# Attention output of a hybrid conv/attention block: the halves of V added on VectorE before the transpose, two heads to a transpose

## The reference

```python
xn = rms_norm(x, norm_mix_g[l])
z = jnp.einsum("bsd,dc->bsc", xn, w_in[l])        # B | C | h | q | k | v
...
scores = jnp.einsum("bnqhd,bnkhd->bnhqk", q, k_band) * (HEAD_DIM ** -0.5) + bias
p = jax.nn.softmax(scores, axis=-1).astype(v.dtype)
o = jnp.einsum("bnhqk,bnkhd->bnqhd", p, v_band)
...
y_mix = concat([group_rms_norm(y_conv, conv_out_g[l], 64), group_rms_norm(y_attn, attn_out_g[l], 64)])
x = x + jnp.einsum("bsc,cd->bsd", y_mix, w_out[l])
xn = rms_norm(x, norm_mlp_g[l])
x = x + relu(xn @ w_mlp_in[l]) ** 2 @ w_mlp_out[l]
```

## Time and profile before

| | |
|---|---|
| median of 3 runs | 1128.45 us (1126.46 to 1129.71) |
| the profiled execution | 1128.77 us, of which its span is 1127.0 us |
| granted PE clock | 0.998 of full speed |
| PE busy | 1101.8 us (98%) |
| PEld busy | 918.2 us (81%) |
| DVE busy | 711.4 us (63%) |
| ACT busy | 538.7 us (48%) |
| POOL busy | 628.5 us (56%) |
| share of PE in the chain that ended last | 91% |

### The profile page before, as it was taken

How to read it: one execution, slowest core, us unless ns; L and a number is a source line. 1 busy time by engine, 2 the same in 40 slices (tenths; PEclk the granted TensorE clock), 3 DMA queues, 4 the chain that set the end, 5 groups by cost and what they waited for, 6 DMA issues and landing times.

```text
span 1127.0 us, 14684 instructions
## 1 busy us (share of the span) xinstructions
PE 1101.8 (98%) x5272; PEld 918.2 (81%) x5272; DVE 711.4 (63%) x899; ACT 538.7 (48%) x885; POOL 628.5 (56%) x368
## 2 busy tenths in 40 slices
PE   5999999999999999999999999999999999999998
PEld 5888888888888877887888888888878888888887
DVE  6677757767766785336425353534467767776798
ACT  6664665565466563225454545445453343333330
POOL 4322141230412130167778888787789697796992
PEclk9999999999999999999999999999999999999999
DMA  8311110120110514121454444444676435345324
GB/s 260 99 38 38 40 56 18 37 58 19 56 38 3 187 71 154 54 78 50 166 195 151 149 150 149 151 148 160 241 281 236 149 121 192 134 132 204 112 75 167
DMA packets 98511, 135.79 MB, mean 120 GB/s; under 512 B 8072, under 2 KB 52112, under 8 KB 98456
## 3 DMA queue, kind: packets, MB, share of 16 engines
q1 hardware_dynamic: 95104, 131.13, 34.7%
q10 hardware_dynamic: 3352, 3.94, 1.2%
HBM read 97.27 MB, written 39.34 MB: 121 GB/s over the span
## 4 chain that ended last, share of the span: by engine, by line
PE 91%; DVE 3%; DMA 2%; ACT 1%; POOL 1%; issue 1%; ACTq 0%; SPq 0%; POOLq 0%; DVEq 0%
PE PJ L1519 22%; PE PJ L1772 10%; PE SC L1772 9%; PE OS L1772 7%; PE PJ L1809 7%; PE PT L1809 7%; PE SC L1809 7%; PE OS L1809 7%; PE PJ L1597 5%; PE OS L1579 2%; PE PT L1566 2%; PE SC L1556 1%; PE SC L1555 1%; DMA gB<-in_norm_mlp_g 1%; DMA xin<-in_x 1%
## 5 line engine op out<-in xcount | busy, mean ns | idle before, releaser
L1519 PE MATMUL PJ<-actT,wsl 128*128 128x512 f32 (+1 forms) x1176 | 296.9, 395 | 0.1
L1519 PEld LDWEIGHTS PJ<-actT,wsl 128*128 128x128 f32 x1176 | 208.8, 189 | 38.0 <-DVE actT L1011 0.5
L614 POOL TENSOR_TENSOR ring<-b,ring 128x1024 fp32r<-128x1024 f32 x48 | 137.6, 2875 | 38.3 <-ACT ring L956 38.2
L1423 DVE TENSOR_TENSOR ring<-hraw,ring 128x1024 fp32r<-128x1024 f32 x56 | 149.7, 2708 | 4.6 <-ACT ring L951 4.6
L505 POOL CAST wsl<-raw 128x1024 fp32r<-128x1024 f32 x24 | 25.9, 1081 | 197.4 <-PE PJ L1519 164.5
L951 ACT ACTIVATE ring<-hraw 128x1024 fp32r<-128x1024 f32 x56 | 59.2, 1057 | 133.4 <-PE OS L1809 60.1
L1772 PE MATMUL OS<-actT,w1a 128*128 128x512 f32 x384 | 93.6, 391 | 0.8 <-ACT p1s L892 0.8
L731 ACT ACTIVATE prob<-prob,negm 128x640 f32<-128x640 f32 (+4 forms) x64 | 44.4, 693 | 90.8 <-DVE negm L1117 90.6
L1809 PE MATMUL PJ<-ring 128*128 128x512 f32 x336 | 82.1, 394 | 2.4 <-POOL ring L614 2.4
L1772 PEld LDWEIGHTS OS<-actT,w1a 128*128 128x128 f32 x384 | 71.6, 188 | 15.7 <-issue 1.2
L1597 PE MATMUL PJ<-wo,actT 128*128 128x512 f32 x336 | 80.1, 393 | 1.5 <-DVE actT L1171 0.8
(11 more groups left out here) (195 smaller groups left out, 2185.4 us busy)
## 6 DMA issues: line engine op xcount, KB each, us to landing
hraw<-hidd SPq DMA_DIRECT2D x56, 512.0 KB, 3.6
w1r<-in_w_mlp_in SPq DMA_DIRECT2D x16, 1024.0 KB, 6.2
hidd<-hs SPq DMA_DIRECT2D x64, 256.0 KB, 2.0
b<-in_w_mlp_out SPq DMA_DIRECT2D x16, 1024.0 KB, 7.2
raw<-in_w_in SPq DMA_DIRECT2D x24, 512.0 KB, 3.8
hidd<-h SPq DMA_DIRECT2D x48, 256.0 KB, 2.3
xin<-in_x SPq DMA_DIRECT2D x8, 512.0 KB, 8.7
woraw<-in_w_out SPq DMA_DIRECT2D x8, 512.0 KB, 8.4
```

What stands on the lines that cost most here:

```text
L614: nc.gpsimd.tensor_tensor(duo(n)[1][LO], W2_SRC[name][:, 2 * d:2 * d + 2], duo(n)[1][HI].bitcast(F32), ALU.subtract).then_inc(s["wl2_done" ...
L1423: vec.tensor_tensor(duo(n)[0][LO], hraw[:, n % HRING], duo(n)[0][HI].bitcast(F32), ALU.subtract).then_inc(s["hl2_done"], 1)
L1519: last = mm(PJ[:, g % 2, cols], wsl[:, w % NSLOT, a, k], actT[:, b, k, c], start=(r == 0), stop=(r == 3 * KD - 1))
```

## The change

`u_sum` becomes two instructions. The first (L1133 of the changed kernel) adds the HI and LO halves of the free dimension, but only for partitions 0 to 63 (V HI). The second (L1135) waits for the first on a new semaphore `fold_done` and adds partitions 64 to 127 (V LO) of the HI half. The LO half of V LO is no longer added. The sum is 64 partitions high: head 0 writes rows 0 to 63 of uT, head 1 rows 64 to 127, so that uT holds both heads of a tile. One transpose (`pair_transpose`) serves two units, and `o_sum` becomes a copy of 128 columns from PSUM. `prob_v` waits in addition until `u_sum` of the unit before is done. The semaphore `acc_zero`, which nothing used, gives its place to `fold_done`.

```diff
             def u_sum(it, u):
 
                 dve.wait_ge(s["pv_done"], it * UNITS + (u + 1))
-                if u >= 2:
-                    dve.wait_ge(s["uq_done"], it * UNITS + (u - 1))
-                vec.tensor_reduce(uT[:, u % 2], UP.rearrange("p b c -> p c b"), AX.X, ALU.add
-                                  ).then_inc(s["us_done"], 1)
+                j, rows = u // 2, HEADS[u % 2]
+                if j >= 2 and u % 2 == 0:
+                    dve.wait_ge(s["uq_done"], it * (UNITS // 2) + j - 1)
+                vec.tensor_reduce(uT[rows, j % 2], UP[0:HD].rearrange("p b c -> p c b"), AX.X, ALU.add).then_inc(s["fold_done"], 1)
+                dve.wait_ge(s["fold_done"], it * UNITS + (u + 1))
+                vec.tensor_tensor(uT[rows, j % 2], UP[HD:P, 0], uT[rows, j % 2], ALU.add).then_inc(s["us_done"], 1)
 
             def o_sum(it, j):
 
-                dve.wait_ge(s["uq_done"], it * UNITS + 2 * (j + 1))
-                vec.tensor_reduce(og[:, j // 4, 2 * (j % 4):2 * (j % 4) + 2], UQ.rearrange("p (u a d) -> p u d a", u=2, a=2),
-                                  AX.X, ALU.add).then_inc(s["oq_done"], 1)
+                dve.wait_ge(s["uq_done"], it * (UNITS // 2) + j + 1)
+                vec.tensor_copy(on[:, j // 4, j % 4 * P:(j % 4 + 1) * P], UQ[:, j % 2 * P:(j % 2 + 1) * P]).then_inc(s["oq_done"], 1)
...
                 if u == 0:
                     pe.wait_ge(s["vlo_done"], it * 2 + 1)
+                if u:
+                    pe.wait_ge(s["us_done"], it * UNITS + u)
...
-            def u_transpose(it, u):
-                pe.wait_ge(s["us_done"], it * UNITS + (u + 1))
-                nc.tensor.transpose(UQ[:, u % 2 * P:(u % 2 + 1) * P], uT[:, u % 2], ident[:, :]).then_inc(s["uq_done"], 1)
+            def pair_transpose(it, j):
+                pe.wait_ge(s["us_done"], it * UNITS + 2 * (j + 1))
+                nc.tensor.transpose(UQ[:, j % 2 * P:(j % 2 + 1) * P], uT[:, j % 2], ident[:, :]).then_inc(s["uq_done"], 1)
...
-                    if u >= 2:
-                        u_transpose(it, u - 2)
+                    if u >= 3 and u % 2:
+                        pair_transpose(it, u // 2 - 1)
...
-                    u_transpose(it, UNITS - 2)
                     prob_v(it, UNITS - 1)
                     fill(8)
-                    u_transpose(it, UNITS - 1)
+                    pair_transpose(it, UNITS // 2 - 1)
...
                     assert n == REST
-                    u_transpose(it, UNITS - 2)
                     prob_v(it, UNITS - 1)
                     sum_squares(it, 5)
                     w_out_both(1, (1,))
-                    u_transpose(it, UNITS - 1)
+                    pair_transpose(it, UNITS // 2 - 1)
```

More of the change, by code:

```diff
@@ L214, in build @@
         b11_in b12_in b21_in b22_in hh2_done wh2_done hl2_done wl2_done ts_done d2_done dr_done
-        acc_in acc_zero fin_done
+        acc_in fold_done fin_done
         """.split()
```

## The result

The changed kernel takes 1136.47 us (median of 6 runs, 1134.03 to 1137.31), against 1128.35 us of the kernel before, measured beside it (6 runs, 1126.46 to 1129.71): ratio 1.0072, 95% interval 1.0061 to 1.0082. It is 8.1 us slower. I had predicted 1127.9 us, within 1125.3 to 1131.4. The profiled execution took 1137.02 us, its span is 1135.2.

The account below looks back on a forecast made before the run. PE was taken to carry 91% of the chain, DVE having slack except at four places. Iterations 0 to 2 at 3 x (-0.76 + 0.16 + 0.37) plus iteration 3's +0.10 gave -0.6 us: 1127.9 us, range 1125.3 to 1131.4.

Parts of the forecast that it names:

- Durations, gaps, overlap: DVE's sum pair: 0.42 us, gap 0.03, add 0.29; the next starts at 0.66, +0.32 a unit or +0.44 where held.
- The transposes: 32 of PE's transposes go, 0.109 us each on the chain; two do not count; 0.76 us saved in iterations 0 to 2 each.
- Step 6 and 7: Two sums on DVE without idle time delay `pt_lo(6)` by 1.00 us; PE waits 0.16 us at `prob_v(6)`, four times.
- DVE's +0.32 in the other steps goes into idle time: Elsewhere DVE's longer sums cost nothing, falling into idle time ahead of L1132 or `pt_lo`.
- my second rival: Step 3: POOL's L508 gets the port before DVE's L1030, 0.8 us in each of four iterations; 1130.9 us; chance 0.25.
- the hold: On DVE, behind half-height instructions on rows 64 to 127 the next starts only at their end: 0.12 us per change of half.
- the 0.14 us of the rival: In step 3, DVE might ask for the port only at its first read, 0.14 us after issue, letting POOL in first.
- End of iterations 0 to 2: DVE's L1049 comes 0.44 us later and POOL's L515 has to let it finish: +0.37 us on the path each time.
- Step 14: Iterations 0 to 2: POOL holds the taps anyway, so DVE's 0.32 us costs nothing; the transpose saved there goes into PE's wait.
- its DVE stretch: Iteration 3 from step 12: the chain runs on DVE through `u_sum(12)` and `u_sum(13)` to `ym_lo(0)`: +0.84 us.
- Iteration 3: Transposes -0.65 and -0.11, step 7 +0.16, DVE from step 12 +0.84, `o_sum(7)` -0.14: +0.10 us in all.

Follow-up runs that it names:

- x3: Changed kernel with `inverse(3, 0)` ahead of `u_sum(4)`, `qk_lo(3)` ahead of `u_sum(5)`, `o_sum(2)` behind the scores, `pair_transpose(2)` behind `score(8)` and three fills: 1135.76 us.
- x5: Changed kernel with the reordering of x3 in steps 5 to 7, and also `qk_lo(2)` at the start of step 5: 1134.28 us.
- x4: Changed kernel with `squares_lo(4)` ahead of `u_sum(9)` in step 10: 1133.88 us.
- x12: Changed kernel with both instructions of every `u_sum` on partitions 0 to 63 alone, leaving out V's low half and the odd units' output places: 1130.07 us.
- x2b: Kernel before, all 64 transposes kept, plus a second reduction of half the columns behind every sum, rewriting the same values: 1131.27 us.
- x10: Changed kernel with transposes of the identity put into PE's two waits at the beginning of step 15 of iteration 3: 1134.21 us.
- x9: Kernel before with the last tap behind `pt_lo(13)` and, in iteration 3, `ym_lo(0)`, `o_sum(6)` and `u_transpose(13)` reordered: 1128.28 us.
- x6: Changed kernel with the orders of x5 and x4, `conv_scale` behind `qk_scale` at iteration ends, and `ym_lo(0)`, `o_sum(6)`, `pair_transpose(6)` moved in iteration 3: 1128.56 us.
- x8: Changed kernel with the orders of x6, but the last tap behind `pt_lo(13)` and `pair_transpose(6)` in the middle of the six output-weight products: 1128.17 us.
- x7: Kernel before with the same orders as x6: 1131.54 us.
- x11: Changed kernel as in x8, with ten transposes of the identity ahead of the first output-weight product of iteration 3: 1126.75 us.

## Why the prediction was wrong

- **Durations, gaps, overlap:** right. 0.417 + 0.03 + 0.293, and the next at 0.66 or 0.77 us; I had 0.66 and 0.78.
- **The transposes:** right. 3.3 us came out of the stretches between the waits (I had said that two of the 32 don't count, but had reckoned with one an iteration, four in all: 28 x 0.109 = 3.05).
- **"Step 6 and 7":** this is the step that failed. I counted 1.00 us of DVE's delay, which is right, and then asked PE's question of one release only, `pt_lo(6)`, at 0.16 us. Between the two sums and `pt_lo(6)` stands `qk_lo(3)`, and `score(8)` waits for it; behind `u_sum(5)` stands the pair's transpose, ahead of that score on PE. The earlier trace rows shows L1059 and no row of mine said who waits for it. It had 0.05 us to spare where the release that I had looked at had 0.84. 4.2 us instead of 0.6; x3 and x5 take the wait away with the order alone.
- **"DVE's +0.32 in the other steps goes into idle time":** wrong in step 10. There my second rival came true, at another place and with 0.57 instead of 0.8 us: L1030 came 0.05 us too late, half the hold. I had looked for the port's order in step 3 alone, because the row there was close; x4 and x12 each took 1.7 us back. In step 3 the order stayed with L1030 issued 0.12 us ahead, and in x2b's step 10 with 0.09, so what decides is who is issued first, and not the 0.14 us of the rival. (Four times its 0.8 is 3.2, not 3.1.)
- **"End of iterations 0 to 2":** the place and the mechanism are right, the size 0.49 and not 0.37.
- **Step 14:** right in that the taps stayed behind POOL. In iteration 3, where POOL doesn't cover them, `prob_v(13)` is 0.48 us later; I had counted this in its DVE stretch.
- **Iteration 3:** mis-sized, +0.10 forecast and +2.7 measured up to `unit_transpose(0)`. The waits are +1.04 before the first product where I had +0.84 from DVE, and step 7 is +0.92 where I had +0.16; the six matmuls at half clock, 1.24 us, were no term at all.
- **Clock:** missing from the sum. In x10's one trace the stretch at 405.9 is gone when PE's waits are filled, so a wait that grows can cost more than itself, 1.24 us here. How often it does isn't shown.
- **The MLP's second half**, +1.7 in the profiled execution, is not explained. x9, a form of the kernel before, has +1.66 there too though it enters that half 0.2 us late; x6, x8 and x2b have +0.2, x7 has -0.55, so it is no result of the change as far as these traces tell.

## What to carry to other kernels

Where a change makes an engine's instruction longer, list for each tight stretch every semaphore that the following instructions release, up to the first idle time, and price each release at its own waiter; here the tensor with the shortest slack was not one that the change touched. Treat slack as a threshold: 0.1 us a unit cost next to nothing alone and about 4 us once another 0.32 us had used the slack up. An order tuned to the old durations belongs to them, so retune it with the change before judging it. Here the change costs 8 us under the old order and gains 3 under the new one; with each kernel in the order that suits it best they are level (x8), or the change is up to 1.8 us ahead (x11), which its interval doesn't quite show.

## What the chip showed that I had not expected

- A 64x64 transpose between full matmuls costs PE 0.29 us more than a 128x128 one that does twice the columns.
- With PE's waits filled by useless transposes the six matmuls behind them took 1.66 us and not 2.93 (x10, one execution).
- DVE's L1030, issued well inside POOL's L508, ended 0.55 us behind it in three traces (before, after, x4), whatever its own length; issued 0.09 (x2b) or 0.12 us (step 3, after) ahead of L508 it went through in 0.68.
- The same kernel spreads over 6 us (x5) with the number of half-clock stretches; runs of one kernel at equal granted clock lie mostly within 2 us of each other, so they compare better than medians of 4 to 6 runs. They leave out what a kernel does to the clock itself.
